# Pairing the blocks of a two-step Fourier transform by distance 1 instead of distance 8

## The reference, cut to what matters

```
def bidir_long_conv(z, h_fwd, h_bwd, bias):
    L = z.shape[1]
    k = jnp.concatenate([h_fwd, jnp.zeros_like(h_fwd[:1]), h_bwd[1:][::-1]], axis=0)
    kf = jnp.fft.rfft(k.astype(jnp.float32), n=2 * L, axis=0)
    zf = jnp.fft.rfft(z.astype(jnp.float32), n=2 * L, axis=1)
    y = jnp.fft.irfft(zf * kf, n=2 * L, axis=1)[:, :L]
    return (y + z.astype(jnp.float32) * bias).astype(z.dtype)
...
    z = v
    for n, gate in enumerate((x1, x2)):
        z = gate * bidir_long_conv(z, filt[:, n, 0], filt[:, n, 1], fbias[n])
```

## Time and profile before

| | |
|---|---|
| time, median of three executions | 3692.31 us (3685.02 to 3703.75) |
| the profiled execution's own time | 3703.75 us |
| its span in the profile | 3701.8 us |
| TensorE (PE) busy | 3364.5 us, 91% |
| VectorE (DVE) busy | 2181.7 us, 59% |
| ScalarE (ACT) busy | 1317.2 us, 36% |
| the stages K, Z, S, M, B | from about 427 to 1100 us of the span |

### The profile page before, as it was taken

How to read it: one execution, slowest core, us unless ns; L and a number is a source line. 1 busy time by engine, 2 the same in 40 slices (tenths; PEclk the granted TensorE clock), 3 DMA queues, 4 the chain that set the end, 5 groups by cost and what they waited for, 6 DMA issues and landing times.

```text
span 3701.8 us, 47892 instructions
## 1 busy us (share of the span) xinstructions
PE 3364.5 (91%) x18246; PEld 2629.2 (71%) x18246; DVE 2181.7 (59%) x3240; ACT 1317.2 (36%) x2215; POOL 314.1 (8%) x510
## 2 busy tenths in 40 slices
PE   3999988888889899999899988999999979999897
PEld 1888645455467688888688866677777758888685
DVE  7998823333336655554486845555655666565676
ACT  2212332332324433333244633333333343333344
POOL 0111233433420000000000200000000000000000
PEclk9999988888979899999999999999999989999999
DMA  6655756765660132222533430000000323332632
GB/s 222 216 197 200 214 120 120 142 135 113 162 219 35 57 117 89 92 83 83 232 98 103 149 121 26 8 7 7 14 24 1 110 86 106 107 100 89 241 99 88
DMA packets 184985, 410.13 MB, mean 111 GB/s; under 512 B 33279, under 2 KB 60223, under 8 KB 183111
## 3 DMA queue, kind: packets, MB, share of 16 engines
q1 hardware_dynamic: 132584, 270.68, 22.2%
q0 software_dynamic: 51936, 131.27, 14.3%
q10 hardware_dynamic: 288, 5.77, 0.4%
HBM read 262.50 MB, written 81.00 MB: 93 GB/s over the span
## 4 chain that ended last, share of the span: by engine, by line
PE 74%; DVE 12%; DMA 8%; ACT 3%; issue 2%; POOL 1%; SPq 0%; DVEq 0%; ACTq 0%
PE ps L618 19%; PE ps L619 19%; PE ps L620 19%; DMA t2w<-w 3%; PE ps L2367 3%; PE ps L2392 3%; PE ps L2240 2%; PE ps L2264 2%; DMA t2z<-s 2%; PE ps L2249 1%; PE ps L688 1%; DVE mx L2758 1%; DMA traw<-hidden_scratch 1%; PE ps L2427 1%; PE ps L2330 1%
## 5 line engine op out<-in xcount | busy, mean ns | idle before, releaser
L618 PE MATMUL ps<-HB,gsp 128*128 128x512 f32 x1232 | 488.7, 397 | 37.2 <-DVE HB L794 21.9
L619 PE MATMUL ps<-HB,gsp 128*128 128x512 f32 x1232 | 485.2, 394 | 0.0
L620 PE MATMUL ps<-HB,gsp 128*128 128x512 f32 x1232 | 483.7, 393 | 0.0
L1072 DVE TENSOR_TENSOR gsp<-graw,gsp 128x512 fp32r<-128x512 f32 x330 | 226.4, 690 | 262.7 <-ACT gsp L1051 262.0
L1051 ACT ACTIVATE gsp<-graw 128x512 fp32r<-128x512 f32 x330 | 206.7, 628 | 326.2 <-PE ps L620 264.9
L618 PEld LDWEIGHTS ps<-HB,gsp 128*128 128x128 f32 x1232 | 234.3, 190 | 90.4 <-issue 21.4
L618 PE MATMUL ps<-tsp,wdh 128*128 128x512 f32 x616 | 244.1, 396 | 35.0 <-DVE tsp L1329 35.0
L620 PEld LDWEIGHTS ps<-HB,gsp 128*128 128x128 f32 x1232 | 234.3, 190 | 50.1
L619 PEld LDWEIGHTS ps<-HB,gsp 128*128 128x128 f32 x1232 | 234.7, 190 | 46.5 <-issue 1.0
L619 PE MATMUL ps<-tsp,wdh 128*128 128x512 f32 x616 | 242.5, 394 | 0.0
L620 PE MATMUL ps<-tsp,wdh 128*128 128x512 f32 x616 | 242.1, 393 | 0.0
(11 more groups left out here) (263 smaller groups left out, 7690.2 us busy)
## 6 DMA issues: line engine op xcount, KB each, us to landing
graw<-in_w_gu SPq DMA_DIRECT2D x176, 256.0 KB, 2.6
mring<-in_mod_w POOLq DMA_DIRECT2D x78, 512.0 KB, 4.6
hidden_scratch<-R SPq DMA_DIRECT2D x154, 256.0 KB, 2.4
traw<-hidden_scratch SPq DMA_DIRECT2D x154, 256.0 KB, 2.6
t2k<-s POOLq DMA_DIRECT2D x80, 256.0 KB, 5.3
t2z<-s POOLq DMA_DIRECT2D x160, 128.0 KB, 5.7
t2w<-w POOLq DMA_DIRECT2D x160, 128.0 KB, 4.5
wd<-in_w_dx SPq DMA_DIRECT2D x6, 2816.0 KB, 14.1
```

Source lines behind the costliest of these rows:

```text
L618: pe.matmul(o, wh, xh, start=start, stop=False, skip_group_check=onto)
L619: pe.matmul(o, wh, xl, start=False, stop=False, skip_group_check=onto)
L620: return pe.matmul(o, wl, xh, start=False, stop=stop, skip_group_check=onto)
L1072: dve.tensor_tensor(gsp[U % 3][:, 1, :], graw[:, q, W_SLOT[i], :], gsp[U % 3][:, 0, :].bitcast(F32), ALU.subtract).then_inc(w.lo, 1)
```

## The change

The second step now pairs block 2y with block 2y+1 instead of block y with y+8. With it go the order in which K makes and sends its blocks and the order in which M sends its blocks. All sizes, counts, engines and waits stay.

```
         def filter_unit(it, half, u):
             e = 8 * half + u
-            return (4 * half + u // 2 + 8 * (u % 2), it, it) if it < NCH else (e % 4, e // 4, NCH + e // 4)
+            return (e, it, it) if it < NCH else (e % 4, e // 4, NCH + e // 4)
...
                         for h in range(2):
-                            g, at = signal_part(it, 2 * (u // 2) + h + 8 * (u % 2))
+                            g, at = signal_part(it, 4 * (u // 2) + 2 * h + u % 2)
                             pool.dma_start(by_partition(t2w, it, g, CW * at, CW), w1[d % 3][:, CW * h:CW * (h + 1)]
...
-                                e = 2 * u + h + 8 * c
+                                e = 4 * u + 2 * h + c
                                 mm = pe.matmul(ps[rows64(c), SETS_S[u % 2] + r, CW * h:CW * (h + 1)],
...
-                                    e = u + 8 * c
+                                    e = 2 * u + c
                                     mm = pe.matmul(ps[rows64(c), SETS_C[u % 2] + r, CW * v:CW * (v + 1)],
...
-                                                   m_[rows64(c), const_at(it, y + 8 * c), 64 * r:64 * r + 64],
+                                                   m_[rows64(c), const_at(it, 2 * y + c), 64 * r:64 * r + 64],
```

## The result

The changed kernel takes 3746.01 us (median of four, 3739.06 to 3752.88) against 3694.02 us before (four executions, 3685.02 to 3703.75): a ratio of 1.0143, 95% interval 1.0115 to 1.0172. It is slower by 52 us; the forecast was 60 us, 3752 us in all.

What follows compares the result with a forecast made beforehand. The prediction took transfer waits in the convolution, from neighbouring blocks sharing a path to SBUF, as the bound. K's 18.6+18.0+11.1 and M's 14.0 made 61.7 us, taken as 60: 3752 us from the 3692.31 median, 8-in-10 range 3704 to 3788.

Steps and rivals of the forecast that it cites:

- the wait for `t2z`: Sign in the chain: waits for Z's transfers after K(it+1,0) should grow by about 6 us.
- the matmul groups: Sign on TensorE: the matmul groups should stay as they were, at cost 0.
- K(1,0), K(2,0), K(3,0): Term for these K stages: last transfer lands 6.2 us later, delaying Z; 3 x 6.2 = 18.6 us.
- 19.5-13.3 = 6.2: Step for K(1,0) and its like: eight transfers' moving time less eight issue periods gives 6.2 us of lateness each.
- K(1,1), K(2,1), K(3,1): Term for K stages behind Z's backlog: 6.0 us each, delaying the following M; 18.0 us.
- the queue hardly runs empty, so the whole difference counts: Step for K(1,1) and its like: from 557 us on, about 13 us becomes 19.5, so 6.0 us each.
- K(0): Term for K(0,0) and K(0,1), run back to back: 16 transfers take 39.0 us instead of 27.9; +11.1 us.
- M: Term for eight M stages: runs of four slow transfers, 1.75 us each, midway between 0 and 3.5; 14.0 us.
- Hidden in K: Rival: K's lateness costs nothing, its 48 us vanish and M's 14 stay; 3706 us, chance 0.13.
- order does not matter: Rival: Z and M move less through smaller transfers and rows; K keeps 196 GB/s; 3692 us, chance 0.09.
- Faster: Rival: only immediate neighbours hinder each other, so M's new pairs gain 20 us; 3672 us, chance 0.04.
- The clock: Rival: longer waits drop TensorE's clock in the four B(it,1), 26 us on top; 3778 us, chance 0.12.

Runs made afterwards that it cites:

- K's part alone: Kernel before with only K's transfers in running order (0 to 7, then 8 to 15): 3741.75 us against 3693.23, ratio 1.0119.
- the one that straddles the groups: Kernel before with K's blocks ordered 3 4 2 5 1 6 0 7, then 11 12 10 13 9 14 8 15: 3695.58 us, ratio 1.0008.
- The falling order: Kernel before with K's blocks sent 7 down to 0, then 15 down to 8: 3747.49 us, ratio 1.0152.
- M alone: Changed kernel with K's transfers back in alternating order, leaving the new pairing and M's new order: 3701.43 us, ratio 1.0030 to before.
- the second comparison: The unmodified changed kernel measured again against the kernel before, for a second trace: 3740.68 us against 3695.93, ratio 1.0117.
- all three stages spread: Kernel before with K, Z and M each sending one block of each group of four in turn: 3645.94 us, ratio 0.9869.
- Z and M spread: Kernel before with Z and M sending one block of each group of four in turn, K left alternating: 3650.69 us, ratio 0.9880.

## Why the prediction was right, and where its terms were off

**The mechanism** held where the loss lies: no engine's work changed, K's transfers slowed on a shared path, and the queue passed their lateness to Z and M. The run with K alone (+44 us) and the one that straddles the groups (no difference, 194 GB/s) show it; neither was to be had from the trace before. I took 108 GB/s for the new order between bounds of 95 and 139, and K(0) ran at 108; that a choice between bounds was met so closely is partly luck. Two signs came otherwise than forecast. Behind K(1,0) the wait for `t2z` grew by 2.4 us and not by 6, and ahead of it stands a new wait for `t2k` of 9.11 us. And the matmul groups did not stay: L2367 gained (below).

**K(1,0), K(2,0), K(3,0)** were forecast at 18.6 us and measured 9.9. The step that was mis-sized is 19.5-13.3 = 6.2. It set the moving time of eight transfers against eight periods of issue. From first issue to last landing the stage took 17.5 us before (its last issue landed in 5.9 us) and takes 21.4 now (9.8 us): +3.9. The 13.3 left out that the last transfer of before has its own flight behind it too. The falling order shows that a change of group at the end hides little more.

**K(1,1), K(2,1), K(3,1)** with the M stages after them were forecast at 18.0 and 5.3 us, and measured 20.8 together. The step "the queue hardly runs empty, so the whole difference counts" held: the first wait for `w1` in M(0,1) grew by 5.6 us.

**K(0)** was forecast at 11.1 us, and the interval up to M(0,0) grew by 21.9. From first issue to last landing it went from 33.5 to 49.7 us, +16.2. In the steady part ScalarE hands over two tiles each 5.2 us or so (451.10, 456.49 and 461.50 us are first issues of such pairs), 101 GB/s; 16 transfers at that rate are 41.5 us, which is 2.5 of the missing 5.1. The rest, and the further 5.7 us up to M(0,0), I can't put down to one cause: Z's transfers share the queue with K's tail there (462 to 478 us).

**M** was forecast at 14.0 us by a guess in the middle, and +11 us (5 to 17) is what its part costs in total. But the traces show two things in it, of which I had only one: slower transfers, and L2367 at the higher clock level. In the ledger this is the -12.0 us of the last line, 10.7 of them L2367's own: 13.88 to 7.33, 13.88 to 11.96 and 13.92 to 11.66 us.

**The rivals.** "Hidden in K" is refuted by K's part alone, "order does not matter" by the same run. The Trainium skill, page "SBUF — State Buffer", section "Can I just issue two DMAs to hit both halves?", has only 6% gained by a second transfer on the other half. That does not carry over to this case: a second path gave 196 GB/s instead of 108. "Faster" by M's new pairs is refuted: M alone is slower. "The clock" moved, and the other way: I had it fall in B(it,1), which kept 7.29 us throughout; it rose in B(it,0).

One row that I set against "order does not matter" was misread. The 213 GB/s of 1013 to 1026 us are not those of the context's M alone. The kernel before in that stretch, by queue (packets, MB, share of the 16 engines):

```profile
q0 software_dynamic: 647, 1.80, 39.9%
q1 hardware_dynamic: 933, 0.94, 21.8%
```

The first is the queue of M's transfers: 138 GB/s at a share of 0.40. The conclusion stands, as that is still more for the share than 196 at 1.05, but the number in the prediction is too high for what it is said to be.

**The sum** was 61.7 us, taken as 60; the medians differ by 52, and by 45 in the second comparison, the pair of traces by 40. Within it errors of both signs stood side by side: in the ledger K(0) is 10.8 us above its term, K(it,0) 8.7 below, and the last line, forecast at +7.0, is 19 below. So the mechanism earned the direction and the rough size; that the sum came within 8 us is partly luck.

**What stays open.** Why B(0,0) runs at the higher level in all three traces with the new order of M, and in none of the other seven. Its matmuls are the same 64; what differs is TensorE's work and idle time ahead of it. In the stretch just before it the granted clock was down in both kernels, 0.50 before (500 to 504 us) and 0.51 after (523 to 527 us), and only the changed kernel has the full one again from its first matmuls on. B(0,0), before and then changed:

```profile
503.50:507.00 3.50, 3.47 (x17) 3.50 (x17) 0.00 (x0) 1.66 (x3) 0.00 (x0) 0.50 0.01 2
...
527.30:531.00 3.70, 3.68 (x33) 3.70 (x34) 0.69 (x1) 1.50 (x3) 0.00 (x0) 1.00 0.01 2
```

The other B(it,0) reach that level without the new order too: 7.36 us in B(2,0) with K in falling order, 7.47 us in B(3,0) with Z and M spread.

## What to carry to other kernels

When a transfer writes only some partitions, ask which ones are in flight together with it: compare the GB/s of two stretches with a DMA share near 1, and make sure by queue that the bytes are those of the transfers in question. Where transfers of equal size move much less at the same share, as here 108 against 196 GB/s, suspect one path, and test it by the order alone: another order of the same transfers, with no work changed, moved this kernel between 3746, 3694 and 3646 us. A stage that keeps up gains nothing from a better order (K), a stage that others wait for does (Z, M).

## What the runs showed of the hardware

A transfer here writes eight partitions, 16 apart. A queue of them whose blocks lie four in a row in one group of four moves 108 GB/s at a DMA share of 1.06, in the changed kernel and with K's part alone. With two groups in turn it moves 196 (0 and 8) and 194 (3 and 4). The 95 GB/s of M's opening before are no clean figure for one group, as its pairs 0 1, 8 9, 2 3 change the group at every second transfer. Four groups in turn gave 197 at a share of 0.87 (583 to 591 us, all three stages spread); what they give at a full share is not shown. The prediction already reckoned by runs of four; that the limit follows the groups so sharply, with 3 and 4 as free of each other as 0 and 8, was shown first by the straddling order. Where on the way to SBUF the limit sits no run shows: the runs changed only which blocks are written one after the other.
